# Two transformer blocks on one core: the arena and the 256-column operands at other SBUF addresses, and the square of a chunk behind the next weight split in the down stages

## The reference, cut to what matters

```python
for l in range(2):                                   # first block
    h  = h  + 0.5 * g1  * swiglu(modulate(rms_norm(h)),  w_ffn1_gate, w_ffn1_up, w_ffn1_down)
    hc = hc + 0.5 * cg1 * swiglu(modulate(rms_norm(hc)), ...)          # the same weights
    p  = modulate(rms_norm(h)) @ w_in                # window, global and neighbourhood attention
    h  = h + gm * (attention(p) @ w_out)
    h  = h + 0.5 * g2 * swiglu(...)                  # hc too, but only in l = 0
h = rms_norm(h)
# second block: rwkv, mla and differential attention from one projection, merged with sigmoid gates,
# then w_o, a convolved feed-forward (1024 -> 2 x 2816 -> 1024) and a last rms_norm
```

## Time and profile before

| | |
|---|---|
| median of 3 runs | 2449.36 us |
| profiled execution, its own time | 2451.35 us |
| its span, first to last instruction | 2450.0 us |
| TensorE matmuls busy | 2318.3 us (95%), 14376 of them |
| VectorE busy | 1496.6 us (61%) |
| ScalarE busy | 966.6 us (39%) |
| GpSimd busy | 360.6 us (15%) |
| mean granted TensorE clock | 0.976 |
| HBM read | 325.56 MB, 134 GB/s over the span |

### The profile page before, as it was taken

The page is one execution under the profiler, slowest core; times in us unless marked ns, Lnnn a source line. Parts: engine busy times, 40 slices in busy tenths (PEclk is TensorE's granted clock), DMA queues, the critical chain, the costliest instruction groups (busy, mean ns, idle before and its releaser), DMA issues. The chain is left out here.

```text
span 2450.0 us, 37074 instructions
## 1 busy us (share of the span) xinstructions
PE 2318.3 (95%) x14376; PEld 1943.1 (79%) x14376; DVE 1496.6 (61%) x2305; ACT 966.6 (39%) x1538; POOL 360.6 (15%) x365
## 2 busy tenths in 40 slices
PE   6999999998999999999999989889998998998998
PEld 4888887665678888778888866579988987898998
DVE  4666656455676765575663364566666656686764
ACT  4222223455442222242222245444436234556762
POOL 1000001000000000000000010069991763000000
PEclk9999999999999999999999999989999998999999
DMA  7554544111135444444442231124453221244444
GB/s 281 177 194 172 174 145 159 69 35 52 61 122 181 177 169 157 138 151 158 173 179 98 100 126 52 52 103 172 169 175 115 104 102 54 90 156 147 169 153 144
DMA packets 52615, 331.05 MB, mean 135 GB/s; under 512 B 6544, under 2 KB 7824, under 8 KB 21648
## 3 DMA queue, kind: packets, MB, share of 16 engines
q1 hardware_dynamic: 49040, 319.15, 36.8%
q0 software_dynamic: 3456, 10.25, 1.4%
HBM read 325.56 MB, written 3.80 MB: 134 GB/s over the span
## 5 line engine op out<-in xcount | busy, mean ns | idle before, releaser
L1161 PE MATMUL bank<-u_hi,whi 128*128 128x512 f32 (+1 forms) x2512 | 872.5, 347 | 38.7 <-DVE u_lo L1115 14.1
L1162 PE MATMUL bank<-u_lo,whi 128*128 128x512 f32 (+1 forms) x2512 | 856.4, 341 | 0.0
L1163 PE MATMUL bank<-u_hi,wlo 128*128 128x512 f32 (+1 forms) x2512 | 856.3, 341 | 0.0
L567 DVE TENSOR_TENSOR wlo<-raw,whi 128x2048 fp32r<-128x2048 f32 (+2 forms) x208 | 434.0, 2087 | 291.3 <-ACT whi L565 291.0
L1161 PEld LDWEIGHTS bank<-u_hi,whi 128*128 128x128 f32 x2512 | 484.4, 193 | 117.9 <-issue 37.0
L1163 PEld LDWEIGHTS bank<-u_hi,wlo 128*128 128x128 f32 x2512 | 483.8, 193 | 51.6
L1162 PEld LDWEIGHTS bank<-u_lo,whi 128*128 128x128 f32 x2512 | 484.8, 193 | 49.8 <-issue 0.2
L565 ACT ACTIVATE whi<-raw 128x2048 fp32r<-128x2048 f32 (+2 forms) x208 | 354.5, 1704 | 157.7 <-DMA raw<-in_stream 96.6
L1223 ACT ACTIVATE sil<-bank 128x512 f32<-128x512 f32 (+1 forms) x88 | 47.9, 544 | 546.6 <-PE bank L1163 546.5
L1161 PE MATMUL bank<-hidden_hi,whi 128*128 128x512 f32 x528 | 209.4, 397 | 4.0 <-DVE wlo L567 4.0
L1163 PE MATMUL bank<-hidden_hi,wlo 128*128 128x512 f32 x528 | 208.6, 395 | 0.0
(11 more groups left out here) (425 smaller groups left out, 3023.2 us busy)
## 6 DMA issues: line engine op xcount, KB each, us to landing
raw<-in_stream SPq DMA_DIRECT2D x231, 1024.0 KB, 4.8
raw<-in_stream SPq DMA_DIRECT2D x80, 704.0 KB, 4.0
first_ada<-in_stream SPq DMA_DIRECT2D x8, 1024.0 KB, 16.7
raw<-in_stream SPq DMA_DIRECT2D x8, 768.0 KB, 4.4
skew<-rpb_rows POOLq DMA_DIRECT2D x8, 336.0 KB, 6.3
nbr_bias<-skew POOLq DMA_DIRECT2D x24, 112.0 KB, 4.0
h<-in_tokens SPq DMA_DIRECT2D x1, 2048.0 KB, 11.8
uq_ukv<-in_small POOLq DMA_DIRECT2D x1, 1536.0 KB, 8.1
```

Of the source, the lines that this page charges most:

```text
L567: v.tensor_tensor(self.lo[to][:, 0:n], raw[:, 0:n], self.hi[to][:, 0:n].bitcast(F32), ALU.subtract).then_inc(self.s_lo, 1)
L1161: pe.q.matmul(dst, w[0], x[0], start=start, stop=False)
L1162: pe.q.matmul(dst, w[0], x[1], start=False, stop=False)
L1163: return pe.q.matmul(dst, w[1], x[0], start=False, stop=stop)
```

## The change

Three things.

1. Homes. A gap is put before the arena so that it starts on the same remainder of 512 bytes as `h`. `u` of the 256-column stages (`u_one`) begins 16 floats (64 bytes) into each row of `u_hi` and `u_lo`; `hidden_x_*` and `hid` begin 64 bytes into the arena. `gates` is cut in two: chunks 0 to 7 stay in `h`, chunks 8 to 23 move 64 bytes up. A spare of 64 bytes (`gates_end`) behind `u_lo` moves `sil`, `prod`, `ssq` and what follows up by 64 bytes.
2. Because of that cut the sigmoid of the gates in the branch stage becomes two instructions, of 256 and 512 columns, where it was one of 768.
3. `run` gets a hook `middle`, called in each group (but the first) after the first panel's matmuls. In the five down stages the square of the last chunk and its addition to `ssq` are taken out of `evacuate` and issued there, so they come behind the split of the group's second panel on both engines.

```diff
+APART = 16
@@ Stream.run
                 multiply(par, part, panel.base % 2).then_inc(self.s_pe, 1)
+                if part == 0 and lag and middle:
+                    middle(prev, 1 - par, prevG)
             if lag and finish:
                 finish(prev, 1 - par, prevG)
@@ build
-    gates = nc.alloc_sbuf_tensor_at("gates", [P, 3 * KC, T], F32, offset=H_AT)[:, :, S:T]
+    u_one = (u_hi[:, :, APART:APART + S], u_lo[:, :, APART:APART + S])
+
+    sb("gates_end", [P, APART])
+    gates_h = nc.alloc_sbuf_tensor_at("gates_h", [P, KC, T], F32, offset=H_AT)[:, :, S:T]
+    gates_u = nc.alloc_sbuf_tensor_at("gates_u", [P, 2 * KC, T], F32, offset=H_AT + KC * T * 4 + 4 * (S + APART))[:, :, 0:S]
...
-    ARENA_AT = (nc.sbuf_base + 31) // 32 * 32
+    ARENA_AT = nc.sbuf_base + (H_AT - nc.sbuf_base) % 512
+    sb("arena_gap", [P, (ARENA_AT - nc.sbuf_base) // 4])
@@ norm
+        to_hi, to_lo = (u_hi, u_lo) if streams == 2 else u_one
...
-    far.at = 0
+    far.at = 4 * APART
     hidden_s = [far.new(f"hidden_x_{n}", [P, FC, S], F32R) for n in ("hi", "lo")]
@@ down
             residual(at(m), banks[2 * par], n, lambda s: gates(m, s)).then_inc(st.s_ev, 1)
+
+        def square(m, par, G):
+            k = Count(q0 + m.base, m.step, m.reg)
+            weighted = vec[:, bass.ds(m.plus(VC.at[weight]), 1)] if weight else None
             act.q.wait_ge(st.s_ev, G.plus(1))
             add_square(at(m), n, count=k, weighted=weighted)
 
-        st.run(name, multiply, evacuate, ppg=2, early=True)
+        st.run(name, multiply, evacuate, ppg=2, early=True, middle=square)
...
-        gate_up(("up2", l), streams * S, ready, u, hid)
+        gate_up(("up2", l), streams * S, ready, u if streams == 2 else u_one, hid)
@@ branch_evac
+        act.q.activation(gates_h[:, c, :], gates_h[:, c, :], ACT.Sigmoid)
         act.q.activation(by_branch[:, :, c, :], by_branch[:, :, c, :], ACT.Sigmoid).then_inc(s_gate, 1)
@@ second block
-    hid2 = [... offset=ARENA_AT + 22528 * i) for i in range(2)]
+    hid2 = [... offset=ARENA_AT + 4 * APART + 22528 * i) for i in range(2)]
...
+    def down2_square(m, par, G):
         act.q.wait_ge(st.s_ev, G.plus(1))
-        add_square(at(m), S, count=k)
+        add_square(at(m), S, count=Count(q0 + m.base, m.step, m.reg))
...
-    st.run("down_2", down2_multiply, down2_evac, ppg=2, early=True)
+    st.run("down_2", down2_multiply, down2_evac, ppg=2, early=True, middle=down2_square)
```

More of the change, by code:

```diff
@@ L623, in split_lo, with run @@
             r.then_inc(self.s_lo, 1)
-    def run(self, name, multiply, evacuate, finish=None, ppg=1, loop=True, second=None, third=None, early=False, ahead=False):
+    def run(self, name, multiply, evacuate, finish=None, ppg=1, loop=True, second=None, third=None, early=False, ahead=False, middle=None):
         ph = PHASE[name]
@@ L1103, in narrow_hi @@
                 B = coeff(c, s)[1]
-                done.append(act.do(act.q.activation(u_hi[columns(c, s)], sil[par][:, i * S:i * S + S], ACT.Identity,
+                done.append(act.do(act.q.activation(to_hi[columns(c, s)], sil[par][:, i * S:i * S + S], ACT.Identity,
                                                     bias=B if B is not None else 0.0)))
@@ L1112, in narrow_lo @@
                 B = coeff(c, s)[1]
-                src, high = sil[par][:, i * S:i * S + S], u_hi[columns(c, s)].bitcast(F32)
-                ready[c] = dve.do(dve.q.tensor_tensor(u_lo[columns(c, s)], src, high, ALU.subtract) if B is None else
-                                  dve.q.scalar_tensor_tensor(out=u_lo[columns(c, s)], in0=src, scalar=B, in1=high,
+                src, high = sil[par][:, i * S:i * S + S], to_hi[columns(c, s)].bitcast(F32)
+                ready[c] = dve.do(dve.q.tensor_tensor(to_lo[columns(c, s)], src, high, ALU.subtract) if B is None else
+                                  dve.q.scalar_tensor_tensor(out=to_lo[columns(c, s)], in0=src, scalar=B, in1=high,
                                                              op0=ALU.add, op1=ALU.subtract))
@@ L1125, in wide_hi @@
             act.after(act_done)
-            return [act.do(act.q.activation(wide(u_hi, g), by_two(sil[par][:, :]), ACT.Copy))]
+            return [act.do(act.q.activation(wide(to_hi, g), by_two(sil[par][:, :]), ACT.Copy))]
         def wide_lo(g, par, done):
             dve.after(done[0])
-            r = dve.do(dve.q.tensor_tensor(wide(u_lo, g), by_two(sil[par][:, :]), wide(u_hi, g).bitcast(F32), ALU.subtract))
+            r = dve.do(dve.q.tensor_tensor(wide(to_lo, g), by_two(sil[par][:, :]), wide(to_hi, g).bitcast(F32), ALU.subtract))
             for c, s in g:
@@ L1886, in pair_multiply @@
     def pair_multiply(par, part, slot):
-        return pair_products(par, slot, u, S, first.pop() if first else None)
+        return pair_products(par, slot, u_one, S, first.pop() if first else None)
     halves = [slice(0, 64), slice(64, 128)]
@@ L1964, in side_quarter @@
                 for b in range(2):
-                    r = three(side_target(0, b), tile_of(slot, b * KC + kc), chunk_of(u, kc, 0, S), kc == 0, kc == KC - 1)
+                    r = three(side_target(0, b), tile_of(slot, b * KC + kc), chunk_of(u_one, kc, 0, S), kc == 0, kc == KC - 1)
         for kc in range(4 * (q % 2), 4 * (q % 2) + 4) if n else ():
@@ L1968, in side_quarter @@
                 w = (whi[slot][:, kc * 256:(kc + 1) * 256], wlo[slot][:, kc * 256:(kc + 1) * 256])
[L1969 removed]
+                r = three(side_target(n, b), chunk_of(u_one, kc, b * P, b * P + P), w, kc == 0, kc == KC - 1)
             else:
[L1971 removed]
+                r = three(side_target(n, b), tile_of(slot, b * KC + kc), chunk_of(u_one, kc, 0, S), kc == 0, kc == KC - 1)
         if q == 3:
@@ L2804, in build @@
     h0 = hidden_count[0]
-    st.run("branch", branch_multiply, branch_evac, finish_hidden(S, (u_hi, u_lo), h0), loop=False)
+    st.run("branch", branch_multiply, branch_evac, finish_hidden(S, u_one, h0), loop=False)
     first.append([(s_hl, hidden_count[0] + c + 1) for c in range(KC)])
@@ L2828, in build @@
     cv = [nc.alloc_sbuf_tensor_at(f"conv_out{i}", [P, 2, S], F32, offset=ARENA_AT + 49152 + 4096 + 8192 * i) for i in range(2)]
-    hid2 = [nc.alloc_sbuf_tensor_at(f"hid2_{i}", [P, FC, S], F32R, offset=ARENA_AT + 22528 * i) for i in range(2)]
+    hid2 = [nc.alloc_sbuf_tensor_at(f"hid2_{i}", [P, FC, S], F32R, offset=ARENA_AT + 4 * APART + 22528 * i) for i in range(2)]
     act.after(*over)
```

24 lines of the change are left out of this document (12 added, 12 removed).

## The result

The changed kernel takes 2412.72 us (median of 4 runs, 2410.82 to 2415.45) beside 2447.26 us for the kernel before in the same session: a ratio of 0.9856, 95% interval 0.9835 to 0.9876, or 34.5 us less. The forecast was 2423.0, range 2402 to 2437. The time lies 10 us under the forecast.

What follows compares the result with a forecast made beforehand. The prediction took matmul step cost and TensorE's waits for low weights as the bounds nearly everywhere. Terms 3.4 + 12.8 + 1.0 + 1.1 + 6.5 + 2.8 = 27.6 us took 2451.35 to 2423.8, adjusted to 2423; range 2402 to 2437.

Steps and rivals of the forecast that it cites:

- The 512-column homes: Down1 of l = 1: `hidden` takes the step of `u`, 6.4 ns less over 527 steps, 3.4 us.
- The rule of two independent ports: 512-column homes: by this rule the address is worth nothing, 3.4 and 1.0 us become zero; that rival's chance 0.10.
- The down stages of l = 0: Both 512-column stages lose their gaps and step 226.7 ns, ending at 119.5 us: 6.4 us each, 12.8 us.
- The loop through the one `raw` buffer: Down stages of l = 0: 7.3 us a panel, holds by 0.2; rival, it takes over, 2433 us, chance 0.08.
- Out of l = 0: Out stage of l = 0: 192 matmuls at 512 columns, 5 to 7 ns less each, 1.0 us.
- The 256-column homes: 256-column stages: 64 bytes from the weights gives a 119.3 ns step for `u`; net 1.1 us gained.
- 64 bytes is a good place: Rival on 256-column homes: `u` steps 115.6 ns, 16.3 us in place of 1.1, 2408 us; chance 0.28.
- their signs: Step of `u` with 256 columns: 119 ns shows the forecast, below 117 the good place, above 121 bad.
- Down2 of l = 1: With the square behind the split, 1.0 of 7.5 us of gaps is let stand: 6.5 us gained.
- Down_2: Of 5.3 us of gaps the 2.4 us wait in the third panel stays: 2.8 us gained.
- W_o and up_2: Counted, with up2 of l = 1, as stages TensorE bounds, 2300 matmuls with `u`; within the net 1.1 us.
- The second sigmoid: Branch stage: 0.42 us for 256 columns, about 0.63 for 512; 1.7 us more on ScalarE, hidden by its wait.

Runs made afterwards that it cites:

- two: Kernel before with only the gap ahead of the arena, squares and `u` as before: 2444.14 us, ratio 0.9984.
- four: Kernel after with `APART = 0`, undoing only the 64 bytes between 256-column operands and weights: 2422.28 us, ratio 0.9895.
- five to eight: Kernel after with other distances of activations from weights, one of the four moving everything up 64 bytes: 2428.98, 2431.82, 2415.55 and 2414.58 us.
- one: Kernel before with the moved squares alone, all homes as before: 2431.02 us, ratio 0.9926.
- three: Kernel after with the squares back in `evacuate`, so the homes alone: 2439.22 us, ratio 0.996.
- s3_all_up_64: Kernel after with 64 bytes put ahead of `raw`, so all operands move up and distances stay: 2415.55 us, one execution.
- v2_silu_table_first, ten: Kernel after with one Silu ahead of up_2's loop, so its table is there on entry: 2417.31 us, ratio 0.988.
- v1_up2_split_first, nine: Kernel after with the next panel's split issued ahead of the last group's evacuation in up_2: 2413.75 us, ratio 0.9858.
- a_again: Kernel after once more, unchanged, as a second set of runs: 2413.48 us, ratio 0.9858.
- twelve: Kernel after with split first and Silu table preloaded in up_2, Sqrt table load behind first splits, 256-column operands at 192 bytes: 2391.81 us, ratio 0.9775.
- x4_apart_0: Kernel after with `APART = 0`, 256-column operands at distance 0 from the weights: 2422.28 us, ratio 0.9895.
- s1_distances: Kernel after with `hidden` at -64 bytes from the weights, `u_one` and `hidden_x` at 32, `hid` at 128: 2428.98 us, one execution.

## Why the prediction was right, and where not

**The 512-column homes** (3.4 us for down1 of l = 1): 3.5. `hidden` took over the step of `u`, 226.7 ns. The rule of two independent ports in the Trainium skill ("TensorE: Matmul & The Clock Gate", "Step-by-step: what each phase is for"), from which the prediction drew that the address is worth nothing, gives no account of this kernel: two, four and five to eight change nothing but addresses, and the step follows. Whether the ports have a part in that no run shows.

**The down stages of l = 0** (12.8): 6.4 and 6.5, both ending at 119.5 us. The step counted in the prediction, copy beside `h` and `wlo` 1.8 us earlier, is what the rows show. Its other half, that neither edit could do this alone, was not said; experiments one to three show it. The loop through the one `raw` buffer held its 0.2 us: no gap came (in the kernel after the `wlo` of panels 968 to 1005 us are 7.25 to 7.39 us apart, TensorE needs 7.48), and the rival that it takes over has fallen. Not foreseen were 2.1 and 1.8 us behind these stages. The first panel of the next stage is loaded into the buffer that the last `wlo` frees. Behind down2 that `wlo`, which before stood behind `ssq`, ended at 1042.37 before, 7.6 us ahead of the stage's last matmul, and at 1021.43 after, 11.4 us ahead. The copy of the new panel, which waits for that load, starts at 1047.17 and 1026.28. So its `wlo` (2.29 us) began at 1049.12 before, 0.9 us ahead of that matmul, and at 1028.23 after, 4.6 us ahead. VectorE takes its work in order, and the last addition to `h`, on which the norm waits, came 1.3 us behind the start of the last matmul before (1051.33) and 0.4 us after (1033.29). Experiment one has this gain too: 6.4 us from stage to stage in both places, against 8.5 and 8.1 before.

**Out of l = 0** (1.0): 0.4. `y_hi` steps 228.3 instead of 232.3 ns (the prediction's row of five steps gave 234). Over 168 undisturbed steps that is 0.7 us; the rest of the stage, in which the attention's products run in between, took 0.3 us back. TensorE waits only some 3 of its 65 us.

**The 256-column homes** (1.1): the term of the sum that was mis-sized. Experiment four gives about 9.5 us against distance 0; `hidden_x` and `hid` stood at 384 bytes before, 1.3 ns better than 0, so against the kernel before I estimate 9.5 - 1054 x 1.3 ns, some 8 us. The forecast took the middle of two known distances, 119.3 ns; `u` came to 117.8, `hidden_x` to 116.4. "Both known distances lie within 1.3 ns" was no ground for what a third would do: of eight places that the trace had not shown six lie below both. The rival "64 bytes is a good place" had the sign right and the size too high: 115.6 forecast, 117.7 measured, 16.3 us against some 8. So the outcome stands between forecast and rival, as the step of `u` does between their signs (119, and below 117).

**Down2 of l = 1** (6.5): 6.7, with 2.1 us of gaps where 1.0 was let stand, and a step 2.3 ns shorter. As foreseen TensorE waits for `wlo` once, 1.2 us, and no more. The copy of a group's second panel starts as the group ends and the square follows it:

```profile
1758.90 1.38 ACT L566 ACTIVATE whi<-raw 128x1408 fp32r<-128x1408 f32 x1 [2.44 <-PE bank L1175]
1760.18 0.40 ACT L979 ACTIVATE prod<-h 128x256 f32 x1
...
1760.31 1.62 DVE L568 TENSOR_TENSOR wlo<-raw,whi 128x1408 fp32r<-128x1408 f32 x1 [0.68 <-ACT whi L566]
```

**Down_2** (2.8): 1.7. The gap in the third panel stayed as said. What comes behind it in this execution is new. Timeline of TensorE:

```profile
2346.14 0.28 PE L1175 MATMUL bank<-hid,wlo 128*128 128x256 f32 x1
2348.95 0.58 PE L1173 MATMUL bank<-hid,whi 128*128 128x256 f32 x1 [2.53 <-DVE wlo L568]
2349.33 0.41 PE L1174 MATMUL bank<-hid,whi 128*128 128x256 f32 x1
2349.54 0.41 PE L1175 MATMUL bank<-hid,wlo 128*128 128x256 f32 x1
...
2351.88 0.28 PE L1174 MATMUL bank<-hid,whi 128*128 128x256 f32 x1
2352.00 0.28 PE L1175 MATMUL bank<-hid,wlo 128*128 128x256 f32 x1
```

Behind the wait 12 steps take 0.21 us each instead of 0.118, at a granted clock of 0.50 (1.2 GHz); it was 1.00 up to the wait, with TensorE at work without a break since the stage began, and is again from 2352. That is 1.1 us, the size of what the forecast misses here. But it belongs to the execution and not to the change. In s3_all_up_64, the same code at the same distances, a wait of the same length after the same unbroken work is followed by full steps at a granted clock of 1.00:

```profile
2349.83 0.39 PE L1174 MATMUL bank<-hid,whi 128*128 128x256 f32 x1 [2.54 <-DVE wlo L568]
2350.06 0.28 PE L1175 MATMUL bank<-hid,whi 128*128 128x256 f32 x1
2350.18 0.28 PE L1176 MATMUL bank<-hid,wlo 128*128 128x256 f32 x1
```

Its down_2 lasts 64.9 us, and that of v2_silu_table_first, also at 1.00, 65.1; with the lower clock it is 66.2 in the kernel after, 66.6 in v1_up2_split_first and 68.0 in a_again. In the kernel before (67.9 us) the clock stayed at 1.00 behind its wait. So without the drop the change brings 2.8 to 3.0 us here, as forecast. Why the clock falls behind this wait in one execution and not in another no run shows.

**W_o and up_2** (counted within the 1.1): nothing, though TensorE's step fell by 2.6 ns over 1248 matmuls, 3.2 us. Here the working was wrong: "2300 matmuls with `u` are in stages that TensorE bounds (up2 of l = 1, w_o, up_2)". Up_2 is bound by the chain of nine, from evacuation to copy to `wlo`: its longer panels last 6.55 us after and 6.56 in four, at 117.8 and at 120.0 ns. Only in twelve, which took that chain away, does a panel last its 48 steps.

**The second sigmoid** takes 616 ns for 512 columns and 404 for 256, near the 0.63 and 0.42 said. It was hidden, as said: the branch lasts 34.9 us in the kernel after, and 35.0 and 34.9 in one and two, which have the single sigmoid.

The sum: 27.6 us forecast, 36.0 in the profiled executions. By stages the 8.4 us between are: 3.9 behind the l = 0 down stages, where nothing was counted; 3.4 in up2 of l = 1 and the second block up to up_2 (1.7 counted there, 5.1 measured); 1.7 in up1, in and up2 of l = 0, where nothing was counted (0.8 of it is the lead at the start of down1, chance as far as the runs tell; for the rest no cause was looked for); 0.2 in the three 512-column down stages; and out, down2 of l = 1 and down_2 together 0.8 less (out 0.6 less, down2 0.5 more, down_2 0.7 less). The forecast's direction and its main terms were right by their mechanism. The range held in part by luck: it had been drawn wide for the 64 bytes, and of the 10 us by which the time undercuts the forecast nearly 4 come from a place where nothing had been counted.

## What to carry to other kernels

Where TensorE is busy without a break, measure start-to-start steps of the same shape with different operands; a difference of a few nanoseconds may be nothing but the distance of the moving operand from the weights (here the table repeats after 256 bytes with 256 columns), and it can be swept with one constant. A gain in the step pays only where TensorE is the bound, so look for stages with waits first and free the chain (in queue order: what the next panel needs before what the next norm needs). Two such edits should be priced together: in the down stages of l = 0 the square alone was worth half and the arena alone a twentieth of what the pair was worth in the same stage. And read a stage in several executions before giving a microsecond of it a cause: down_2 of the same code differs by 3 us.

## What the runs showed of the hardware

- The step of a matmul with its own weight load depends on the distance of the two operands in SBUF: from 113.3 to 120.0 ns at 256 columns, from 226.7 to 233.3 ns at 512. Moving all operands 64 bytes up together changes nothing (s3); other moves of that kind were not run.
- At some distances there are two paces, 117.8 and 113.3 ns, each held over hundreds of steps. The same code can run at either: up2 of l = 1 lasts 127.1 us in v1_up2_split_first and 128.7 in the kernel after.
- At a granted clock of 0.50 (1.2 GHz) the 256-column step is 213 ns, just 256 columns at that clock, and it is so in down_2 at 64 bytes (after), at 0 (x4_apart_0) and at 128 (s1_distances) alike; at 2.4 GHz it is 106.7 ns for the columns and 7 to 13 ns more. So in these stretches the part beyond the columns, and with it the distance, only shows at the full clock.
- Behind one and the same wait of 2.5 us in down_2 the granted clock falls to 0.50 in one execution (after) and stays at 1.00 in another (s3), with 12 long steps or none.
- A table load takes 1283 ns on ScalarE, as "ScalarE: Activation LUTs" in the Trainium skill says in "What ACT_TABLE_LOAD costs"; of the drain of 1380 ns that the section adds, this trace shows nothing: the copy ahead of it ends at 2263.35 and Silu starts at 2264.66. A load can stand in every round of a loop because the table on entry differs from that on coming back, and then one function ahead of the loop removes it (ten).
